# A modulation matrix through TensorE's column groups, one DiT layer on one core

## The reference

```python
sc_lat, sc_ctx = silu(c), silu(c_ctx)
mod_l = split(sc_lat @ w_ada + b_ada, 6)        # w_ada: 2048 x 12288
mod_c = split(sc_ctx @ w_ada + b_ada, 6)        # of these only shift and scale of the first norm are used
n_lat = modulate(rmsnorm(x, g_norm1), mod_l[0], mod_l[1])
n_ctx = modulate(rmsnorm(ctx, g_norm1), mod_c[0], mod_c[1])
z = n @ w_in                                    # then S5 mixer, LRU mixer
m = sigmoid(z_ga) * (ya @ w_proj_a) + sigmoid(z_gb) * (yb @ w_proj_b)
h = x + mod_l[2] * (m @ w_out)
out = rmsnorm(h + mod_l[5] * peer_ffn(modulate(rmsnorm(h, g_norm2), mod_l[3], mod_l[4])), g_final)
```

## Time and profile before

| | |
|---|---|
| median of 3 runs | 2794.79 us (2794.18 to 2798.1) |
| span of the profiled execution | 2788.0 us |
| what lies around the span, against the median | 6.8 us |
| TensorE busy | 2296.5 us, 82% |
| VectorE busy | 1581.9 us, 57% |
| POOL busy | 1089.8 us, 39% |
| ScalarE busy | 421.5 us, 15% |
| DMA | 793.48 MB, mean 285 GB/s |

### The profile page before, as it was taken

How to read it: one execution, slowest core, us unless ns; L and a number is a source line. 1 busy time by engine, 2 the same in 40 slices (tenths; PEclk the granted TensorE clock), 3 DMA queues, 4 the chain that set the end, 5 groups by cost and what they waited for, 6 DMA issues and landing times.

```text
span 2788.0 us, 20854 instructions
## 1 busy us (share of the span) xinstructions
PE 2296.5 (82%) x7608; PEld 1326.9 (48%) x7608; DVE 1581.9 (57%) x2443; ACT 421.5 (15%) x788; POOL 1089.8 (39%) x905
## 2 busy tenths in 40 slices
PE   5989689899988897897987898777777777777777
PEld 2344235776666766786874444222222222222223
DVE  4425570499999996112166545565655566656441
ACT  3023430112222211000011111101111111011101
POOL 3000001446655564000026444555555555455541
PEclk9999899998888886998998999999999999999999
DMA  9931113866666664466469999999999999999995
GB/s 268 325 104 45 45 57 115 218 207 200 200 197 190 189 193 133 135 193 240 154 220 411 414 404 421 421 422 421 421 421 422 421 421 422 421 422 421 421 419 205
DMA packets 315205, 793.48 MB, mean 285 GB/s; under 512 B 25736, under 2 KB 243088, under 8 KB 247264
## 3 DMA queue, kind: packets, MB, share of 16 engines
q0 software_dynamic: 81600, 561.36, 49.5%
q1 hardware_dynamic: 223712, 225.55, 25.8%
q10 hardware_dynamic: 9792, 5.25, 0.8%
HBM read 778.40 MB, written 9.50 MB: 283 GB/s over the span
## 4 chain that ended last, share of the span: by engine, by line
DMA 32%; PE 15%; DVE 3%; POOL 3%; issue 2%; ACT 0%; DVEq 0%; ACTq 0%; POOLq 0%
DMA vb<-in_peer_v,eidx 29%; PE ps L1532 8%; PE ps L1479 4%; PE ps L1504 2%; DMA rows<-in_peer_u,eidx 1%; DMA mT<-in_peer_u,eidx 1%; POOL vb L1247 1%; POOL rows L1247 1%; POOL mT L1247 1%; DMA cut<-in_peer_sub_keys 0%; DVE rows L1439 0%; PE ps L1489 0%; PE ps L1514 0%; DVE mT L1439 0%; DVE oh L1400 0%
## 5 line engine op out<-in xcount | busy, mean ns | idle before, releaser
L1532 PE MATMUL ps<-vb,diag 128*128 128x512 f32 x2048 | 953.0, 612 | 286.1 <-DMA vb<-in_peer_v,eidx 280.9
L1532 PEld LDWEIGHTS ps<-vb,diag 128*128 128x128 f32 x2048 | 377.4, 193 | 859.2 <-DMA vb<-in_peer_v,eidx 449.8
L1439 DVE CUSTOM_DVE_ANT_0 rows<-rows,f 128x2048 f32<-128x2048 f32 x170 | 387.5, 2291 | 334.2 <-DMA rows<-in_peer_u,eidx 333.8
L1247 POOL DMA_INDIRECT vb<-in_peer_v,eidx x256 | 366.9, 1433 | 491.9 <-PE ps L1532 473.1
L989 PE MATMUL ps<-nT,w_ring 128*128 128x256 f32 (+1 forms) x1792 | 538.7, 464 | 2.3 <-issue 1.6
L989 PEld LDWEIGHTS ps<-nT,w_ring 128*128 128x128 f32 x1792 | 361.9, 204 | 186.5 <-issue 144.0
L1439 DVE CUSTOM_DVE_ANT_0 mT<-mT,f 128x2048 f32<-128x2048 f32 x86 | 196.4, 2291 | 176.6 <-DMA mT<-in_peer_u,eidx 176.5
L1247 POOL DMA_INDIRECT rows<-in_peer_u,eidx x170 | 214.4, 1261 | 98.5 <-DVE hd L1439 50.6
L906 DVE SCALAR_TENSOR_TENSOR zu<-w_ring,scol,zu 128x256 f32<-128x256 f32 x448 | 206.3, 524 | 2.3
L1323 ACT ACTIVATE diag<-ident,wgt 128x128 f32<-128x128 f32 x256 | 94.1, 397 | 656.9 <-PE ps L1532 651.7
L1247 POOL DMA_INDIRECT mT<-in_peer_u,eidx x86 | 102.2, 1188 | 211.1 <-DVE eidx L1409 161.6
(11 more groups left out here) (326 smaller groups left out, 2092.5 us busy)
## 6 DMA issues: line engine op xcount, KB each, us to landing
w_ring<-in_w_ada SPq DMA_DIRECT2D x96, 1024.0 KB, 9.8
w_ring<-in_w_in SPq DMA_DIRECT2D x56, 1024.0 KB, 5.3
w_ring<-in_w_out SPq DMA_DIRECT2D x16, 1024.0 KB, 5.7
w_ring<-in_peer_w_query SPq DMA_DIRECT2D x16, 1024.0 KB, 13.7
w_ring<-in_w_proj_a SPq DMA_DIRECT2D x8, 1024.0 KB, 5.9
w_ring<-in_w_proj_b SPq DMA_DIRECT2D x8, 1024.0 KB, 5.7
gates_dram<-gst POOLq DMA_DIRECT2D x16, 256.0 KB, 6.4
big<-big SPq DMA_DIRECT2D x128, 32.0 KB, 5.4
```

Of the source, the lines that this page charges most:

```text
L1247: pool.indirect_dma_start(ring[m % n], None, table, bass.IndirectOffsetOnAxis(ap=eidx[:, i % 3, j:j + 1], axis=0))\
L1439: v.tensor_tensor_reduce(ub[m % n_u], ub[m % n_u], f[:, i // HEADS], 1.0, 0.0, ALU.mult, ALU.add, hd[:, i % 2, j:j + 1]).then_inc(u_used, 1)
L1532: last = pe.matmul(ps[:, 4 * tile + c, :], diag[:, m % NDIAG], vb[m % NV][:, c * 512:(c + 1) * 512], start=(r == 0), stop=(r == HEADS * K ...
```

## The change

The matrix goes through TensorE everywhere. A unit of w_ada is now 4 blocks of 128 rows by 512 columns (pieces of 2 KB), four units make a column block. `scol` is widened to 32 columns per block (two used, the rest zero); the block j of a unit writes to the output partitions 32j to 32j+31, so each of the four blocks has a column group of the array, and the four partial sums of a column block stand in one PSUM bank. ScalarE copies the bank to `part` (it takes the place of `ada_acc` in `zu`), and a matmul with a selector `sel` (128x2, ones at the partitions 32g and 32g+1) adds the four groups up. In the front `part` is the stationary operand and `sel` moves (`mod_columns`): the result comes out as columns in bank 7, so there is no store, no read-back and no transpose. In the stages `sel` is the stationary operand, and the row goes to `modst` and `mods_dram` as before. In a stage TensorE runs the four units between `s5_params(s)` and `s5_states(s-1)`; VectorE's `modulations` are gone. VectorE copies `Cc` earlier and `pwb`, `pP` later. The accumulators are renumbered; the count of units and their places in the ring stay.

```diff
+        def plan_ada(q, count):
+            for x in range(4):
+                src = w_ada[:, 4 * x:4 * x + 4, q * ADA:(q + 1) * ADA]
...
+def ada_view(slot):
+
+    return slot.rearrange("p k n -> p (k n)").rearrange("p (k n) -> p k n", n=ADA)
...
-        ada_acc = zu.rearrange("p b s c -> p (b s c)").rearrange("p (j e n) -> p j e n", j=2, e=2)
-        ones = sb("ones", [P, 1])
+        part = zu.rearrange("p b s c -> p b (s c)")
...
-            for q in range(8):
-                store_mods(q)
-            for j, (row, m) in enumerate(((0, 0), (0, 1), (1, 0), (1, 1))):
-                pool.dma_start(mrow[16 * j:16 * j + 16], mods_dram[row, m * D:(m + 1) * D]
-                               .rearrange("(k p) -> k p", p=P)).then_inc(mrow_back, 16)
...
-            for c in range(16):
-                mod_rows(A0 + c, c)
+            for q in range(8):
+                act.wait_ge(acc_full, A0 + q + 1)
+                if q >= 2:
+                    act.wait_ge(sel_done, q - 1)
+                act.activation(part[:, q % 2], ps[:, (A0 + q) % 2, :], ACT.Copy).then_inc(acc_free, 1)
...
+            def mod_parts(s):
+                a = S0 + 4 * s + 2
+                act.wait_ge(acc_full, a + 1)
+                if s == 0:
+                    act.wait_ge(u_out, 16 * KW)
+                act.activation(part[:, s % 2], ps[:, a % 2, :], ACT.Copy).then_inc(acc_free, 1)
...
             def mod_sums(s):
-                a = S0 + 3 * s + 2
+                a = S0 + 4 * s + 3
                 act.wait_ge(acc_full, a + 1)
-                act.wait_ge(mods_out, 16 * (8 + s - 1))
+                if s >= 2:
+                    act.wait_ge(mods_out, 16 * (s - 1))
...
+            v.wait_ge(sel_done, 8)
+            step(v.tensor_copy(mcol.rearrange("p m k r -> p (m k r)"), ps[:, 7, 0:4 * KD]))
...
-            def modulations(s, units_of):
...
-                    modulations(s, (0, 1))
                     build_m(s)
-                    modulations(s, (2, 3))
...
             def mods(a):
 
                 free(a)
-                for h_ in range(2):
-                    w = unit(pe, n[0])
+                for x in range(4):
+                    w = ada_view(unit(pe, n[0]))
                     n[0] += 1
-                    for k in range(UK):
-                        last = pe.matmul(ps[0:2, a % 2, 0:COLS], sc[:, h_ * UK + k, :], w[:, k, :],
-                                         start=(h_ + k == 0), stop=(h_ * UK + k == KD - 1))
-                    last.then_inc(unit_done if h_ == 0 else acc_full, 1)
+                    for j in range(4):
+                        last = pe.matmul(ps[32 * j:32 * j + 32, a % 2, :], scol[:, 4 * x + j, :], w[:, j, :],
+                                         start=(x == 0), stop=(x == 3))
+                    last.then_inc(ada_used if x < 3 else acc_full, 1)
+
+            def mod_columns(q):
+
+                pe.wait_ge(acc_free, A0 + q + 1)
+                if q == 0:
+                    pe.wait_ge(s5_setup, 4)
+                for i in range(4):
+                    c = 2 * (4 * q + i)
+                    last = pe.matmul(ps[:, 7, c:c + 2], part[:, q % 2, i * P:(i + 1) * P], sel[:], start=True, stop=True)
+                last.then_inc(sel_done, 1)
...
-            for c in range(16):
-                mods(A0 + c)
-
-            pe.wait_ge(mrow_in, 16 * 2)
-            pe.wait_ge(mrow_back, 16 * 4)
-            pe.wait_ge(s5_setup, 4)
-            pe.transpose(ps[:, 2, 0:112], mrow[:], ident[0:112, 0:112]).then_inc(mcol_tr, 1)
+            for q in range(8):
+                mods(A0 + q)
+                if q >= 1:
+                    mod_columns(q - 1)
+            mod_columns(7)
...
-                    n[0] += 4
                     s5_params(s)
+                    mods(S0 + 4 * s + 2)
                 else:
                     s5_out(s - 2)
                 if 1 <= s <= NSTAGE:
                     s5_states(s - 1)
                 if s < NSTAGE:
-                    a = S0 + 3 * s + 2
+                    a = S0 + 4 * s + 3
                     free(a)
-                    pe.wait_ge(ada_used, 4 * s + 4)
-                    for e in range(2):
-                        last = pe.matmul(ps[0:1, a % 2, :], ones[:], ada_acc[:, :, e, :], start=(e == 0), stop=(e == 1))
-                    last.then_inc(acc_full, 1)
+                    pe.wait_ge(acc_free, a)
+                    pe.matmul(ps[0:1, a % 2, :], sel[:, 0:1], part[:, s % 2], start=True, stop=True)\
+                        .then_inc(acc_full, 1)
```

More of the change, by code:

```diff
@@ L89, in build @@
         acc = 0
-        for c in range(16):
+        n_ada = [0]
+        def plan_ada(q, count):
+            for x in range(4):
+                src = w_ada[:, 4 * x:4 * x + 4, q * ADA:(q + 1) * ADA]
+                if x < 3:
+                    n_ada[0] += 1
+                    units.append((src, ada_used, n_ada[0]))
+                else:
+                    units.append((src, acc_full, count))
+        for q in range(8):
             acc += 1
-            plan_pair(w_ada, c, acc_full, acc)
+            plan_ada(q, acc)
         for first in (W // COLS, 0):
@@ L102, in build @@
             plan_pair(w_in, 3 * W // COLS + s, acc_full, acc)
-            acc += 1
-            for x in range(4):
-                w = w_ada[:, (x % 2) * UK:(x % 2 + 1) * UK]
-                c = 16 + 2 * s + x // 2
-                units.append((w[:, :, c * COLS:(c + 1) * COLS], ada_used, 4 * s + x + 1))
+            acc += 2
+            plan_ada(8 + s, acc - 1)
         for c in range(W // COLS):
@@ L122, in load_unit @@
                 eng.wait_ge(units[u - RING][1], units[u - RING][2])
-            eng.dma_start(w_ring[:, u % RING], units[u][0]).then_inc(w_in_sem[u % RING], 16)
+            slot = w_ring[:, u % RING]
+            if units[u][0].shape[1] == 4:
+                slot = ada_view(slot)
+            eng.dma_start(slot, units[u][0]).then_inc(w_in_sem[u % RING], 16)
         def unit(pe, u):
@@ L616, in _ @@
                     evac_pt(s)
+                if s < NSTAGE:
+                    mod_parts(s)
                 if 1 <= s <= NSTAGE:
@@ L676, in _ @@
             step(v.tensor_copy(dT[:], ps[0:H, 3, 2 * G:3 * G]))
+            v.wait_ge(tr_s5, 2)
+            for b in range(4):
+                v.tensor_copy(Cc[:, b // 2, (b % 2) * 32:(b % 2) * 32 + 32, :].rearrange("p g h -> p (g h)"),
+                              ps[:, 4 + b, :]).then_inc(s5_setup, 1)
+            v.wait_ge(s5_setup, 4)
             v.wait_ge(dt_done, 1)
@@ L758, in _ @@
             chain(ea, 8, er, ei)
+            v.wait_ge(sel_done, 8)
+            step(v.tensor_copy(mcol.rearrange("p m k r -> p (m k r)"), ps[:, 7, 0:4 * KD]))
+            for x in range(2):
+                step(tt(nshift[:, x], mcol[:, 0, :, x], bcol[:, 0:16], ALU.add))
+                step(tt(nscale[:, x], mcol[:, 1, :, x], bcol[:, 16:32], ALU.add))
+                step(tsc(nscale[:, x], nscale[:, x], 1.0, None, ALU.add))
+                if x == 0:
+                    step(tt(nscale[:, x], nscale[:, x], bcol[:, 32:48], ALU.mult))
+                else:
+                    tt(nscale[:, x], nscale[:, x], bcol[:, 32:48], ALU.mult).then_inc(norm_ready, 1)
+            for k in range(KD):
+                v.wait_ge(nt_tr, k + 1)
+                tsc(nT[:, k, T:2 * T], ps[:, 4 + k % 2, 0:T], nscale[:, 0, k:k + 1], nshift[:, 0, k:k + 1],
+                    ALU.mult, ALU.add).then_inc(nt_lat, 1)
             step(v.memset(pwb[:], 0.0))
@@ L1094, in _ @@
                 if s < NSTAGE:
-                    two = columns(S0 + 3 * s, T, 2 * T)
+                    two = columns(S0 + 4 * s, T, 2 * T)
                     next(two)
```

100 lines of the change are left out of this document (31 added, 69 removed).

## The result

| | before | after |
|---|---|---|
| median (4 runs each, same chip) | 2794.61 us (2794.18 to 2798.1) | 2760.52 us (2755.58 to 2761.19) |
| ratio, 95% interval | | 0.9876 [0.9862, 0.989] |
| span of the profiled execution | 2788.0 us | 2759.4 us |

The change makes the kernel 34 us faster. The forecast was 2810 us, slower by 15, so the direction was wrong. That the result lies 0.5 us inside the lower end of the range, 2760, is luck: the end was set there for rival B, and the forecast's own range began at 2789. The text gave "faster" a third. The traces differ by 28.6 us, the medians by 34.1. A run of after with a span of 2759.4 us took 2761.19, so 1.8 lie around a span.

The account below looks back on a forecast made before the run. It took TensorE to bound the front and the TensorE-VectorE ping-pong the stages: front -27, fourteen turns +38, stage 1 +4.4, together +15.4 us on 2794.8, so 2810 us; range 2760 to 2845.

Parts of the forecast that it names:

- rival B: Stages: all four column groups run at once, mods 3.5 us plus 0.4, turn 35.9, total 2768 us; chance 0.24.
- The bound and the front: Up to norm_ready: the bound moves from TensorE to the DMA at 380 GB/s, norm_ready 135.3, 27 us less.
- The 54.5 us at which unit 4 was put: Front: start of unit 4, counted back from 151.3 us; from it unit 31 was to land at 129.0.
- The price of a 128x512 matmul into 32 columns: Stages: only neighbouring groups overlap in pairs, so a stage's 32 mods records take 7.7 us, between bounds 3.5 and 13.85.
- hand-overs and s5_out 7.0: Last terms of the stage turn: s5_out 7.0 us, an average of the earlier trace, and hand-overs 0.4, within 38.4.
- rival D: Stages: pairs overlap and mods keep the clock high to s5_out's end; turn 37.1, total 2792 us; chance 0.12.
- The mode change of 0.35: Stages: TensorE changing back from 32-column to 128-column output adds some 0.35 us, included in the 7.7 of mods.
- The end of the turn: From s5_states to s5_out: TensorE's selector and column group 7.8 us against VectorE's copy wait and scan 7.6; 7.8 taken.
- TensorE's way: Between s5_states and s5_out: selector 0.9 plus first column group 6.9, 7.8 us in all.
- Stages 0 and 1: First two stages, without s5_out: stage 0 unchanged, stage 1 from 24.5 to 28.9 us, +4.4.
- the same end: Stage 0: the new selector follows later, about 555.6, but lasts 0.9 and not 3.6 us, so no change.
- worth only 1.4 us a turn: Stages: removing VectorE's 16.8 us of sums per stage shortens a turn only from 35.6 to 34.2 us.

Follow-up runs that it names:

- short_pieces: Kernel after, with each unit of w_ada loaded by two DMAs of 256 columns (1 KB pieces); 2764.24 us.
- two_runs: Kernel after, with blocks 0, 1, 2, 3 of a unit sent to two column groups in the order 0, 0, 1, 1; 2777.38 us (one run).
- pb_once: Kernel after, with POOL's build_pb left out for stages 1 to 15 but for one small operation; 2730.22 us.
- thin_mods: Kernel after, with only 32 of the 512 columns of each block multiplied in the stages, loads and waits kept; 2747.45 us.
- before_params: Kernel after, with all four units of a stage's mods moved ahead of s5_params; 2805.8 us.
- pb_first: Kernel after, with POOL's build_pb(s+1) moved ahead of the three stores of a turn; 2728.01 us.

## Why the prediction was wrong

**The bound and the front: right.** A shift at the stages' end carries through nearly one for one (33 us at the selector of stage 15, 30 at the first gather, 29 at the end). The front went from TensorE to the DMA; forecast 380 GB/s and norm_ready at 135.3, measured 387 and 135.5. short_pieces shows that the rate is the longer pieces' doing. The 54.5 us at which unit 4 was put and the 6.3 us behind the last load had no such test, and norm_ready varies by 8 us between executions of the same front. The matmuls of the front would have fitted in the loads' time even with two groups (two_runs: norm_ready 133.7).

**"The price of a 128x512 matmul into 32 columns": this step failed.** It took "The two records of one matmul use the same columns, so the second has to follow the first; if records start in order, the first record of group j+1 can only run beside the second of group j", and from it 7.7 us a stage. Measured are 3.64, at the lower bound of 3.5. The assumption about the order had no row behind it. The two bounds had, and between them the argument chose. The turn was forecast 2.9 us too long (38.4 against 35.5): this term alone is 4.1 too long and s5_out 0.5, and the end of the turn is 1.6 too short; both are told of below. The price scales with the number of groups, 13.92, 7.08 and 3.64, whatever the order of the two-group runs.

**"hand-overs and s5_out 7.0": the second error.** two_runs tests the sum with mods of nearly the size it took, 7.1 us. With 7.1 in place of 7.7 the forecast is 37.8 a turn and about 2800 us, and that of rival D 36.5 a turn; two_runs measured 36.5 and 2777 us. The scan, forecast at 6.3, was 5.64, and s5_out, forecast at 7.0, was 5.48, with a granted clock of 0.92 over the turns where before had 0.85. The average of the earlier trace rows held the lower clock of before in it. So even with mods of 7.1 us the sum would have come out 23 us too high, and what D described was there in two_runs. In after the clock gave less back: s5_out took 6.47.

**The mode change of 0.35: not seen as an extra.** Params, mods and the gap ahead of s5_states take 7.94 us in after and 4.27 in before; 3.67 more, of which the mods are 3.64, and s5_states begins at 722.12, as the last record of the mods ends (718.55 + 3.64). The 0.40 us gap stands where it stood, ahead of L1060, and none was added.

**The end of the turn: wrong side.** The earlier trace rows gives the undisturbed scan 5.56 us (1084.24 + 0.28 less 1078.96) and not 5.35, as pb_once measured it too. "TensorE's way" was to lead with 7.8; it took 8.1 (725.02 + 7.16 less 722.12 + 2.00), and VectorE's led with 1.42 + 7.99 = 9.4. The scan, forecast at 6.3, took 8.0: the shorter mods bring it 4 us closer to the start of build_pb, of which it then meets more.

**Stages 0 and 1.** "the same end" in stage 0 was 6.1 us better than the front alone gives, 33.2 against 27.1, of which some 4 are the shorter mods; stage 1 grew by 3.1, forecast 4.4, though its mods too were 4.1 shorter than priced.

**What rival B said.** Four groups at once, turn 35.9, 2768 us. Its turn was 35.5, its mechanism is what happened, and so is its place of the loss: VectorE's 16.8 us per stage are worth little. That they are "worth only 1.4 us a turn" was, if anything, too much: a turn without them and with hardly any mods (thin_mods) takes 35.2 us, not 34.2, as the wait for the ring slot and the lower clock behind it come in. The rest of what was to be had lay in two places, one that the forecast took as given (build_pb beside the scan) and one that it did not name for the stages (when a ring slot comes free).

## What to carry to other kernels

Here TensorE and VectorE wait for each other in turn. Work that is taken off an engine buys little where it lay in the shadow of such an exchange, but it leaves a hole, and the gain comes when something is moved into it: here 34 us with the change, 67 with one reordering on POOL, and that reordering alone loses 55. So look what else contends for the freed engine's time before and after, and price an edit of the order on each of two orders, not on one.

Where a price lies between two bounds a factor of four apart, and no row decides, the forecast is the choice between them: weigh it as two cases. And a mean duration from a kernel in which the engine pauses isn't the duration in one in which it doesn't.

## What the runs showed of the hardware

- Matmuls of 128x512 float32 into 32 output columns run side by side in different column groups: 32 records in 13.92 us with one group, 7.08 or 7.06 with two in either order, 3.64 with four; the starts within a four are 6.6 ns apart.
- DMA with pieces of 2 KB moved 387 GB/s into the ring from 60 to 120 us of the span, with pieces of 1 KB 349.
- POOL's tensor operations beside VectorE's: VectorE's 128x512 with two inputs takes 0.69 us alone and 1.5 beside (L891, 3.03 for two), the scan 5.6 us or up to 10.3, 14 scaled sums 7.1 with little of POOL's beside them and 12.2 beside build_pb.
- The last 16 records of s5_out took 1.97 us at a granted clock of 1.00 and 3.62 at 0.50. After waits of 1.6 to 3.8 us ahead of s5_out they took 3.62 (the turns shown of after and before_params), and after thin_mods' waits of some 3 us the column group of 7.15 us took 9.2. But pb_first shows 3.62 in a turn without such a wait, so the wait alone doesn't decide it.
